# Splitting a float32 product into high and low parts: two half-width terms turned into one 512-column matmul, with the work cut into half panels

## The reference, cut to what matters

```python
u = rmsnorm(x, g_mlp) @ w_up                       # [256, 2048] @ [2048, 8192]
return x + jnp.square(jax.nn.relu(u)) @ w_down     # [256, 8192] @ [8192, 2048]
...
proj = x @ w_in                                    # fox: 2048 -> 3 * 2048 + 16
q, k, v, f_pre = jnp.split(proj, [D_MODEL, 2 * D_MODEL, 3 * D_MODEL], axis=-1)
```

## Time and profile before

| | |
|---|---|
| median of 3 runs | 2299.94 us (2298.53 to 2301.85) |
| span of the profiled execution | 2299.5 us; its own time is not given beside it, so sums are made against this span, 0.4 us under the median |
| PE busy | 98% of the span; weight loads 88% |
| DVE busy / ACT busy | 53% / 41% |
| granted TensorE clock | 0.996 of full, mean over the span |
| DMA | 179 GB/s, 55% of the 16 engines' time on SP's queue |

### The profile page before, as it was taken

How to read it: one execution, slowest core, us unless ns; L and a number is a source line. 1 busy time by engine, 2 the same in 40 slices (tenths; PEclk the granted TensorE clock), 3 DMA queues, 4 the chain that set the end, 5 groups by cost and what they waited for, 6 DMA issues and landing times.

```text
span 2299.5 us, 32304 instructions
## 1 busy us (share of the span) xinstructions
PE 2264.5 (98%) x14211; PEld 2026.6 (88%) x14211; DVE 1207.9 (53%) x1164; ACT 946.2 (41%) x900; POOL 12.3 (1%) x34
## 2 busy tenths in 40 slices
PE   7999999999999999999999999999999999999997
PEld 7988778999988899988899987889998889999886
DVE  5688665545444354545445544555546444545444
ACT  5453564444433343433333334534435333344332
POOL 1000000000000000000000000000000000000000
PEclk9999999999999999999999999999999999999999
DMA  8445435666555566555555444555665555665553
GB/s 257 153 156 167 154 128 186 199 183 182 184 191 193 183 183 182 184 193 184 188 181 171 164 163 150 175 191 165 183 183 186 196 186 183 185 184 187 195 183 128
DMA packets 210844, 412.12 MB, mean 179 GB/s; under 512 B 12740, under 2 KB 12832, under 8 KB 210096
## 3 DMA queue, kind: packets, MB, share of 16 engines
q1 hardware_dynamic: 210304, 409.89, 55.3%
q0 software_dynamic: 432, 0.62, 0.2%
HBM read 408.39 MB, written 2.10 MB: 179 GB/s over the span
## 4 chain that ended last, share of the span: by engine, by line
PE 98%; DVE 1%; ACT 1%; DMA 0%; issue 0%; DVEq 0%; SPq 0%; ACTq 0%
PE bank L1680 16%; PE bank L1681 16%; PE bank L1682 16%; PE bank L1694 15%; PE bank L1697 15%; PE bank L1696 15%; PE bank L1769 1%; PE bank L1709 1%; PE bank L1794 0%; PE bank L1803 0%; PE bank L1888 0%; PE bank L1862 0%; PE bank L1781 0%; PE bank L1773 0%; PE bank L1795 0%; DMA G<-in_g_mix_dram 0%
## 5 line engine op out<-in xcount | busy, mean ns | idle before, releaser
L930 DVE TENSOR_TENSOR wl<-raw,wh 128x2048 fp32r<-128x2048 f32 x380 | 870.2, 2291 | 647.7 <-ACT wh L494 645.3
L494 ACT ACTIVATE wh<-raw 128x2048 fp32r<-128x2048 f32 x380 | 726.6, 1913 | 724.4 <-DMA raw<-in_mlp_w_dram 263.8
L1694 PE MATMUL bank<-XH,wh 128*128 128x256 f32 x2880 | 818.4, 284 | 0.0
L1697 PE MATMUL bank<-XH,wl 128*128 128x256 f32 x2880 | 813.2, 282 | 0.0
L1696 PE MATMUL bank<-XL,wh 128*128 128x256 f32 x2880 | 810.8, 282 | 0.0
L1696 PEld LDWEIGHTS bank<-XL,wh 128*128 128x128 f32 x2880 | 547.9, 190 | 0.6 <-issue 0.5
L1694 PEld LDWEIGHTS bank<-XH,wh 128*128 128x128 f32 x2880 | 544.4, 189 | 3.6 <-issue 2.1
L1697 PEld LDWEIGHTS bank<-XH,wl 128*128 128x128 f32 x2880 | 543.3, 189 | 0.0
L1682 PE MATMUL bank<-wh,hl 128*128 128x512 f32 x1024 | 404.5, 395 | 0.0
L1681 PE MATMUL bank<-wl,hh 128*128 128x512 f32 x1024 | 404.4, 395 | 0.0
L1680 PE MATMUL bank<-wh,hh 128*128 128x512 f32 x1024 | 402.2, 393 | 0.0
(11 more groups left out here) (302 smaller groups left out, 818.9 us busy)
## 6 DMA issues: line engine op xcount, KB each, us to landing
raw<-in_mlp_w_dram SPq DMA_DIRECT2D x128, 1024.0 KB, 5.4
raw<-in_w_up_dram SPq DMA_DIRECT2D x64, 1024.0 KB, 5.5
raw<-in_w_down_dram SPq DMA_DIRECT2D x64, 1024.0 KB, 5.1
raw<-in_fox_w_in_dram SPq DMA_DIRECT2D x48, 1024.0 KB, 5.1
raw<-in_w_in_dram SPq DMA_DIRECT2D x44, 1024.0 KB, 5.0
raw<-in_w_out_dram SPq DMA_DIRECT2D x16, 1024.0 KB, 5.0
raw<-in_fox_w_out_dram SPq DMA_DIRECT2D x16, 1024.0 KB, 5.1
G<-in_norm_g_dram SPq DMA_DIRECT2D x4, 1024.0 KB, 5.7
```

The source lines that it names most:

```text
L494: act.activation(wh[:, j, :, :], raw[:, j, :, :], ACT.Copy).then_inc(hi_ready, 1)
L930: dve.tensor_tensor(wl[:, j, :, :], raw[:, j, :, :], wh[:, j, :, :].bitcast(F32), ALU.subtract)\
L1694: pe.matmul(o, sh, mh, start=first and kk == 0 and f % 2 == 0, stop=False, skip_group_check=True)
L1697: mm = pe.matmul(o, sl, mh, start=False, stop=last and kk == 3, skip_group_check=True)
```

## The change

It does three things to 37 of the 45 turned panels: all of the MLPs' first product but the first panel of each MLP (30), and fox q and k but the first panel (7).

1. XH and XL become one tile `XHL`, in which the high and the low row of a block stand side by side. A stationary `wh` block takes both as one moving operand of 512 columns: XH·wh lands in the left half of a bank, XL·wh in the right half. XH·wl is added to the left half by a matmul of 256 columns.
2. A result block now fills a whole bank, so a pair of banks holds 256 output columns, not 512. A chunk is 1 MB of 8 input blocks x 256 columns in place of 4 x 512 (`half_panels`; runs of 1 KB in HBM in place of 2 KB), and a pair of banks is emptied after every second chunk.
3. When a pair is emptied the halves are added. MLP: ACT copies the right halves to `LP`, DVE adds the left halves from the banks, then one instruction does ReLU and square; high and low part follow, all at 256 columns. Fox: ACT copies the right halves into `FQ`/`FK`, DVE adds the left halves and scales.

The loops over panels are written out, and counts of `acc_freed` are adjusted.

```diff
+            def half_cols(b, o):
+                for j in range(4):
+                    x, e = o + j // 2, j % 2
+                    if e == 0:
+                        acc_wait(x)
+                    pe.wait_ge(lo_ready, 4 * b + j + 1)
+                    for kk in range(8):
+                        k = 8 * e + kk
+                        at = 256 * (kk % 2)
+                        for f in range(2):
+                            bk = acc[x % 2][f]
+                            sh, sl = (z[:, j, kk // 2, at + f * P:at + (f + 1) * P] for z in (wh, wl))
+                            pe.matmul(bk[:, :].rearrange("p (s t) -> p s t", s=2), sh, XHL[:, k, :, :],
+                                      start=k == 0, stop=False, skip_group_check=True)
+                            mm = pe.matmul(bk[:, 0:TOK], sl, XH[:, k, :], start=False, stop=k == KT - 1,
+                                           skip_group_check=True)
+                    mm.then_inc(chunk_used, 1)
+                    yield j
...
+                def part(u, o, b, j):                      # ACT, MLP
+                    act.wait_ge(chunk_used, 4 * b + j + 1)
+                    for k in range(2):
+                        act.wait_ge(sq_ready, 2 * u)
+                        act.activation(LP[:, k, :], acc[o % 2][k][:, TOK:], ACT.Copy).then_inc(part_ready, 1)
...
+            def fox_part(n, j):                            # ACT
+                acc_o = fox_acc(n) + j // 2
+                act.wait_ge(chunk_used, 4 * (B_FOX + n) + j + 1)
+                kind, f = FOX[n][0], 4 * (n // 2) + j - 1
+                for k in range(2):
+                    dst = FQ if kind == "fq" else FK
+                    act.activation(dst[:, f + k, :], acc[acc_o % 2][k][:, TOK:], ACT.Copy)\
+                       .then_inc(step["fqk_part"], 1)
...
             def fox_side(n):                               # in ACT and in DVE, first in the slot
+                if 1 <= n // 4 <= 8 and n % 4 in (0, 2):
+                    p, e = n // 4 - (n % 4 == 0), 3 if n % 4 == 0 else 1
+                    if 1 <= p <= 7:
+                        fox_part(p, e)
...
+            def fox_part(n, j):                            # DVE
+                for k in range(2):
+                    dve.wait_ge(step["fqk_part"], 4 * n - 4 + j - 1 + k + 1)
+                    dve.tensor_tensor(dst[:, f + k, :], acc[acc_o % 2][k][:, 0:TOK], dst[:, f + k, :], ALU.add)\
+                       .then_inc(acc_freed[acc_o % 2][k], 1)
+                for k in range(2):
+                    dve.wait_ge(acc_freed[acc_o % 2][k], acc_o // 2 + 1)
+                dve.scalar_tensor_tensor(out=dst[:, f:f + 2, :], in0=dst[:, f:f + 2, :],
```

More of the change, by code:

```diff
@@ L367, in mlp @@
                     b = b0 + half * B_HALF
-                    panel(w_a, b, 0, half * HALF)
+                    if half == 0:
+                        panel(w_a, b, 0, half * HALF)
+                    else:
+                        half_panels(w_a, b, half * HALF)
                     if half == 0:
                         gain(next_gain, used)
[L371 to L376, removed]
+                    for n in range(1, UP):
+                        half_panels(w_a, b + n, half * HALF + 512 * n)
                     for n in range(DOWN):
@@ L403, in _ @@
             for n, (kind, col) in enumerate(FOX):
-                panel(fox_w_in[0], B_FOX + n, 0, col)
+                if kind in TFORM and n:
+                    half_panels(fox_w_in[0], B_FOX + n, col)
+                else:
+                    panel(fox_w_in[0], B_FOX + n, 0, col)
                 if n == 0:
@@ L579, in mlp @@
             def mlp(b0, o0, u0, which):
[L582 to L602, removed]
-                for half in range(2):
[L605 to L616, removed]
+                def whole(u, o, b):
+                    act.wait_ge(chunk_used, 4 * b + 4)
+                    for k in range(2):
+                        act.wait_ge(hl_ready, 2 * u + k + 1)
+                        act.activation(RB[:, k, :], acc[o % 2][k][:, :], ACT.Relu).then_inc(acc_freed[o % 2][k], 1)
@@ new lines, in hidden @@
+                def hidden(j, half, n, b):
+                    if j >= 2:
+                        if half == 0 and n == 0:
+                            return
+                        u, e, wide, tile = up_acc(half, n), 1, False, 4 * n
+                    else:
+                        n, b = n - 1, b - 1
+                        if n < 0:
+                            return
+                        u, e, wide, tile = up_acc(half, n + 1) - 1, 3, half == 0 and n == 0, 4 * n + 2
+                        if wide:
+                            tile = 4 * n
+                    o, u = o0 + half * O_HALF + u, u0 + half * U_HALF[0] + u
+                    if j % 2:
+                        high(u, tile, wide)
+                    elif wide:
+                        whole(u, o, b)
+                    else:
+                        part(u, o, b, e)
@@ L1093, in hidden @@
[L1093 to L1100, removed]
-                for half in range(2):
[L1103 to L1111, removed]
-                    for j in range(4):
-                        lo(b + UP - 1, j)
-                        if m == 3 and half == 0:
-                            fox_added(j)
-                        hidden(j, u + UP - 2, (o + UP - 2) % 2, (o + UP - 2) // 2 + 1, 4 * (UP - 2))
@@ L1117, in mlp @@
+                for half in range(2):
+                    b, od = b0 + half * B_HALF, o0 + half * O_HALF + O_DOWN[half]
+                    for n in range(UP):
+                        for j in range(4):
+                            if n or j >= (2 if half else 3):
+                                lo(b + n, j)
+                            if m == 3 and half == 0 and n == UP - 1:
+                                fox_added(j)
+                            hidden(j, half, n)
                     for n in range(DOWN):
@@ L1964, in _ @@
             for n, (kind, col) in enumerate(FOX):
-                if n:
-                    panel(cols if kind in TFORM else rows, B_FOX + n, O_FOX + n, FOX_AT, 4 * n)
+                if n and kind in TFORM:
+                    for j in half_cols(B_FOX + n, fox_acc(n)):
+                        side_work(FOX_AT, 4 * n + j)
+                elif n:
+                    panel(rows, B_FOX + n, fox_acc(n), FOX_AT, 4 * n)
             acc_wait(O_FOUT)
```

179 lines of the change are left out of this document (123 added, 56 removed).

## The result

The change makes the kernel slower: 2324.99 us (median of 4, 2323.84 to 2327.63) beside 2300.89 for the kernel before (median of 4), ratio 1.0109 with the interval 1.0097 to 1.0121. That is 14.5 us above the forecast and 5 above the top of its range.

A forecast was written before the change was run, and what follows sets the result against it. PE, busy for 98% of the span, was taken to bound the kernel. 2299.5 - 14.4 (matmuls) + 22.6 (fox stalls) + 2.5 (clock) = 2310.2, stated as 2310.5 us, range 2304.5 to 2314 (chance 0.60).

The forecast's parts named there:

- the clock term: Clock falls at fox's eight stalls: one or two expected, 1.7 us each, +2.5 us; none to eight would be 0 to 13.6.
- the two "gaps" of the earlier trace: Clock falls before the change: behind 3.4 us with 1.47 us of transposes, and 3.4 us of nothing; stall called shorter.
- the stalls come and the clock falls at most of them: Rival on fox's stalls: 2307.7 plus 8 to 14, so 2316 to 2322 us; chance 0.12.
- Part 2: Fox: PE waits for probabilities behind DVE's half-panel emptying, eight stalls of 2.83 us, +22.6 us (19 to 26).
- Part 1: Matmuls of 37 turned panels: merging gains 6.1 ns in each of 2368 groups, -14.4 us (13.3 to 15.6).
- the row form's 232 ns: Pace of 512-column matmuls in row-form windows, 231.4 to 232.4 ns, taken for the merged matmul in turned panels.
- Parts 3 and 4: MLPs' emptying costs nothing while 0.54 us to spare holds; 148 chunks in 1 KB runs by DMA cost nothing.
- the rival on DMA and the 0.54 us: Rival: 1 KB packets cost +89 us, or slower ACT/DVE hand-over in MLPs 6 us per further 0.1 us; chance 0.05.

The follow-up runs named there:

- The runs with shorter gaps: Changed kernel with 8, 6 or 4 extra matmuls ahead of each of eight waits, or probabilities between DVE's additions and scaling: 2309.25, 2309.75, 2316.86, 2316.05 us.
- filled: Changed kernel with 11 unused matmuls of 512 columns on PE ahead of each of the eight waits for probabilities: 2308.25 us, ratio 1.0036.
- probabilities first: Changed kernel with DVE taking the probabilities ahead of the half panel's emptying in fox's slots 18 to 32: 2286.34 us, ratio 0.9940.
- the kernel before with its stall: Kernel before, with DVE scaling the whole panel ahead of the probabilities in fox's slots 20, 24, 28 and 32: 2313.58 us, ratio 1.0055.

## Why the prediction was wrong

**The step that failed is the clock term**, "I take one or two, +2.5 us". There were six falls, and three of them lasted 6.8 us and not 3.4, so that the term measured 14.1 us in the spans and 16.7 in the medians. It was mis-sized twice.

The number of falls came from likening a stall of 2.83 us to the two "gaps" of the earlier trace rows, and from the argument that over 10 us of full work lie between two stalls. But 3.4 us is the length of the stretches for which those rows give sums, and not of a gap. In the kernel before, PE stood for 4.66 us ahead of the second fall, and ahead of the first only in pieces of 0.40, 0.73 and 1.28 us:

```profile
316.21 1.06 PE L1810 MATMUL bank<-ident,Y 128*128 128x128 f32 x8 [0.40 <-DVE Y L1356]
318.01 1.09 PE L1810 MATMUL bank<-ident,Y 128*128 128x128 f32 x8 [0.73 <-ACT PTm L552]
320.38 0.76 PE L1680 MATMUL bank<-wh,XH 128*128 128x512 f32 x1 [1.28 <-DVE XL L938]
```

So a pause shorter than 2.83 us was no argument against a fall. The runs with shorter gaps show that the full work between stalls is no cover either: at 1.95 us five stalls of eight still made the clock fall.

The price of one fall, 1.7 us, was that of the first fall in the trace. The second, of which the earlier trace rows show only what came ahead of it, was twice as long:

```profile
1555.90:1562.70 6.80, 5.56 (x25) 0.50 0.19 74
```

The rival "the stalls come and the clock falls at most of them" named the mechanism, had a chance of 0.12, and its upper end was 2322, since it too took 3.4 us for every fall. Its sum with the measured 30.6 us at half clock would have been 2307.7 + 15.3 = 2323, where the span was 2322.1 and the median 2325. That a fall can last 6.8 us could be read in the trace of before; how many stalls would bring one could not. Even the same pieces of idle time near 320 us bring a fall in nine of the twelve profiled executions of this document and none in three. The fault was to give such a term the value near its lower end.

**Part 2 was right.** Eight stalls of 2.83 us, 22.6, were measured as 2.97 and 23.4 (filled against probabilities first). No link was off by more than 0.10: ACT began 0.10 earlier, and PE followed DVE's probabilities in 0.14 and not 0.05. Heads 8 and on did not wait.

**Part 1 was right in its total, and partly by luck in how it is made up.** -14.4 was forecast, and -14.9 (spans) and -13.5 (medians) measured. In the MLPs a group gained 5.5 ns where 6.1 was taken: its pace went from 357.0 to 351.4 ns, at the upper end of the 350.4 to 351.4 forecast. From one start to the next, the matmul of 512 columns takes 234.0 ns there and the one of 256 behind it 118.0 (medians in the trace), so the row form's 232 ns was a good row to go by, 2 ns too low. In fox a group gained 8.6 ns, which nothing in the prediction explains, and 0.6 us is the fall behind fox, which now reaches less far into the MLP; 10.5, 3.9 and 0.6 make up the 14.9 to 0.1. The Trainium skill, page "TensorE: Matmul & The Clock Gate", section "Back-to-back issue gap", adds 2.5 ns to the columns of each isolated matmul at full clock, so that one matmul less saves 2.5 ns; the trace does not agree.

**Parts 3 and 4 were right.** `hi` began 0.54 us after ACT's first copy, as forecast, 0.65 us were to spare for 0.54, a half panel took 11.25 us (32 groups of 351.6 ns), and PE waited for `wl` nowhere. 1 KB runs landed in 5.5 us with q1 at 54.6% (55.3% before). So the rival on DMA and the 0.54 us fell, and the Trainium skill's page "DMA: Bandwidth & Descriptors", section "Specifications", has transfers of 512 bytes or more at line rate; the trace agrees in so far as runs of 1 KB cost no more time than runs of 2 KB.

**The sum.** 2299.5 - 14.9 + 23.4 + 14.1 = 2322.1, the span. What stays open: why three falls of the six last twice as long, and why two stalls of the eight make none. One thing is in the traces: of the 22 falls at stalls of fox in all of these kernels, the four long ones began between 0.1 us ahead of PE's going on and 0.6 behind it, and the 18 short ones 0.9 to 2.1 us behind it. The falls outside of fox do not all follow this: the one near 320 us began 0.13 us ahead (320.25 and 320.38) and lasted 3.4.

## What to carry to other kernels

When an emptying, a copy or a scaling is put on an engine's queue, look at what comes right behind it there, and which engine has that result next in its own order: here an emptying ahead of the probabilities cost 37.5 us, and behind them nothing. Price a short idle gap of TensorE, repeated after every second chunk, by its length plus the clock: gaps of 2 to 3 us cost some 0.4 to 0.7 of their length on top here (the kernel before with its stall 3.5 us by the medians or 6.4 by the spans on 9.2, the change 14.1 or 16.7 on 23.8), and filling one with other work of PE, or leaving only 1 us of it, took that part away. When a trace shows how often the clock fell and for how long, go through all of its falls, and take the idle time in the timeline and not in a window. Before a change is given up for being slower, see which of its parts it is: this one is worth 13.5 us with two steps exchanged (2286.34 us).

## What the runs showed of the hardware

- The clock fell at short gaps of PE with over 10 us of matmuls between two of them: 0 of 8 at 1.03 us, 1 of 8 at 1.49, 5 of 8 at 1.95, 7 of 8 at 2.35 and 6 of 8 at 2.97, each counted in one execution. A fall was 3.4 or 6.8 us long. Near 320 us the same three pieces of idle time, up to 1.3 us each among transposes, brought a fall in nine executions of twelve.
- At half clock a pair of 512 and 256 columns starts every 0.64 us, and at full clock every 0.351, so a fall costs a little under half of its length: 14.1 us of 30.6.
- 24 transposes, back to back, kept the clock up as 11 matmuls did (2308.8 and 2308.25 us, no fall in either).
- Merging two matmuls of 256 columns of float32 rows into one of 512, with the same weights, saved 5.5 ns in the MLPs and 8.6 in fox, 6.1 on the mean (5.1 by the medians of the runs), with 234.0 ns from the start of one of 512 to the next matmul.
